# Stick-breaking attention heads: the running sum's row copied by ScalarE straight into the operand, in place of a copy by ScalarE and one by GpSimd

## What is computed

```python
z = jnp.einsum('bqhd,bkhd->bhqk', q_blk, kh).astype(jnp.float32) * scale
mask = key_pos[None, :] < q_pos[:, None]
log_1m_beta = jnp.where(mask, jax.nn.log_sigmoid(-z), 0.0)
between = lax.cumsum(log_1m_beta, axis=3, reverse=True) - log_1m_beta
weights = jnp.where(mask, jnp.exp(jax.nn.log_sigmoid(z) + between), 0.0)
return jnp.einsum('bhqk,bkhd->bqhd', weights.astype(vh.dtype), vh)
```

## Time and profile before

| | us |
|---|---|
| median of three runs | 1421.17 |
| the three runs | 1421.07, 1421.17, 1424.47 |
| profiled execution | 1422.15 |
| its span | 1420.4 |
| mean granted TensorE clock | 0.985 |

### The profile page before, as it was taken

One profiled execution on the slowest core, in us unless ns is written; L12 is line 12 of the kernel. 1 busy time (PEld: TensorE's weight loads), 2 busy tenths in 40 slices (PEclk: granted clock), 3 DMA queues, 4 the chain that ended last, 5 costly groups with the idle time before them and its releaser, 6 DMA issues.

```text
span 1420.4 us, 27700 instructions
## 1 busy us (share of the span) xinstructions
PE 1355.1 (95%) x11020; PEld 1062.2 (75%) x11020; DVE 873.6 (61%) x1347; ACT 676.3 (48%) x1249; POOL 322.2 (23%) x434
## 2 busy tenths in 40 slices
PE   6999989999899999998999889999999999999997
PEld 5877767877677665655578678888888888888886
DVE  6245261475753465667376787766766656668866
ACT  5533241252523487978464544454444434345541
POOL 6675544532332042435103100000000000000000
PEclk9999999999999899999999999999999999999999
DMA  6555333522325330403253254454444865787952
GB/s 206 148 156 151 104 82 89 152 67 72 95 75 126 124 77 2 91 2 121 85 180 104 82 161 145 147 163 148 156 141 161 294 198 175 253 277 246 298 193 112
DMA packets 191546, 201.07 MB, mean 142 GB/s; under 512 B 36669, under 2 KB 127994, under 8 KB 191418
## 3 DMA queue, kind: packets, MB, share of 16 engines
q1 hardware_dynamic: 145132, 169.47, 37.8%
q10 hardware_dynamic: 46286, 29.84, 7.5%
HBM read 145.06 MB, written 54.20 MB: 140 GB/s over the span
## 4 chain that ended last, share of the span: by engine, by line
PE 44%; DVE 3%; ACT 1%; DMA 1%; issue 1%; DVEq 0%; SPq 0%; ACTq 0%
PE all_ps_b L2670 20%; PE all_ps_b L2661 19%; PE all_ps_b L1669 4%; DMA pl_slot<-in_w_out 1%; PE all_ps_b L2617 0%; DMA pl_xt<-in_w_ff 0%; DVE ro_slot L2325 0%; DVE pl_hH L2511 0%; DVE pl_hL L2511 0%; DVE ro_hT L2325 0%; DVE pl_y L2305 0%; DVE pl_y L2307 0%; DVE ro_wo L2329 0%; ACT pl_hL L2239 0%; DVE pl_xt L2349 0%
## 5 line engine op out<-in xcount | busy, mean ns | idle before, releaser
L484 POOL TENSOR_TENSOR fr_wL<-fr_raw,fr_wH 128x256 fp32r<-128x256 f32 (+1 forms) x208 | 162.5, 812 | 75.1 <-PE fr_ps_F L1278 53.8
L1278 PE MATMUL fr_ps_F<-fr_hL,fr_wH 128*128 128x512 f32 (+1 forms) x416 | 168.2, 404 | 2.9 <-DVE fr_hL L805 2.4
L1278 PE MATMUL fr_ps_F<-fr_hH,fr_wH 128*128 128x512 f32 (+1 forms) x416 | 166.1, 399 | 0.0
L1278 PE MATMUL fr_ps_F<-fr_hH,fr_wL 128*128 128x512 f32 (+1 forms) x416 | 111.6, 397 | 0.7 <-POOL fr_wL L484 0.7
L2661 PE MATMUL all_ps_b<-ro_hH,ro_slot 128*128 128x512 f32 x272 | 89.7, 397 | 5.9 <-ACT pl_raw L2139 5.9
L1278 PEld LDWEIGHTS fr_ps_F<-fr_hL,fr_wH 128*128 128x128 f32 (+1 forms) x416 | 76.6, 184 | 22.8 <-issue 3.1
L1278 PEld LDWEIGHTS fr_ps_F<-fr_hH,fr_wL 128*128 128x128 f32 (+1 forms) x416 | 75.1, 184 | 19.9 <-issue 1.5
L1278 PEld LDWEIGHTS fr_ps_F<-fr_hH,fr_wH 128*128 128x128 f32 (+1 forms) x416 | 76.7, 184 | 17.6 <-issue 1.3
L478 POOL CAST fr_wH<-fr_raw 128x1024 fp32r<-128x1024 f32 (+1 forms) x42 | 47.5, 1130 | 161.2 <-PE fr_ps_F L1278 141.1
L2670 PE MATMUL all_ps_b<-ro_hH 128*128 128x512 f32 x312 | 75.9, 389 | 0.0
L2670 PE MATMUL all_ps_b<-ro_y 128*128 128x512 f32 x300 | 72.7, 390 | 0.5 <-DVE ro_y L2489 0.5
(11 more groups left out here) (483 smaller groups left out, 3114.7 us busy)
## 6 DMA issues: line engine op xcount, KB each, us to landing
pl_slot<-in_w_ff SPq DMA_DIRECT2D x88, 256.0 KB, 4.5
pl_slot<-second_operands SPq DMA_DIRECT2D x75, 256.0 KB, 3.6
fr_raw<-in_w_in ACTq DMA_DIRECT2D x37, 512.0 KB, 4.2
second_operands<-pl_hL SPq DMA_DIRECT2D x64, 256.0 KB, 2.0
pl_hT<-in_w_ff SPq DMA_DIRECT2D x44, 256.0 KB, 4.6
projected<-fr_stage ACTq DMA_DIRECT2D x39, 256.0 KB, 4.4
pl_hT<-second_operands SPq DMA_DIRECT2D x37, 256.0 KB, 3.7
pl_xt<-in_w_ff SPq DMA_DIRECT2D x16, 512.0 KB, 5.6
```

The costliest lines, as they stand in the source:

```text
L484: m = pool.tensor_tensor(wL[b][:, k:k + 2, 0:wd], raw[b][:, k:k + 2, 0:wd], wH[b][:, k:k + 2, 0:wd].bitcast(F32), ALU.subtract)
L1278: m = pe.matmul(F[b][0:wd, :], w[b][:, k, 0:wd], a[:, k, :], start=(at_ == 0), stop=(at_ == len(passes) - 1))
```

## The change

The row buffers are gone. ScalarE copies row 0 of the bank straight into row 0 of `SP[(u + 2) % 4]`. For that it has to wait until the softplus of unit u+2 is done (`sp`), since that one writes the same buffer. The copy's place in ScalarE's queue moves: it was between the weight of unit u and the Exp of unit u+3, and is now between the Exp and the Ln of unit u+3. In the last units of a pair, where there is no unit u+3, it stands right behind the weight. The semaphore `handed` is gone; the scores wait for `placed`, at the same counts. GpSimd keeps its other work and has no row copies.

```diff
-        row = [r.sb(f"row{n}", [1, HALF]) for n in range(4)]
@@ GpSimd
                     if not first:
-                        known = UNITS[u - 2][3]
-                        pool.wait_ge(s("handed"), handed(i, u - 2))
-                        pool.wait_ge(s("sp"), i * NU + u + 1)
-                        pool.tensor_copy(SP[u % 4][0:1, known:HALF], row[(u - 2) % 4][0:1, known:HALF]
-                                         ).then_inc(s("placed"), 1)
                         gla(i * NG + NTH[u] - 1)
@@ ScalarE
             def logs(i, u):
+                exponential(i, u)
+                logarithm(i, u)
+
+            def exponential(i, u):
                 act.wait_ge(s("z"), i * NU + u + 1)
                 if u >= 4 or i:
                     act.wait_ge(s("tri_mm"), i * NU + u - 3)
                 act.activation(part(E[u % 4], u), part(Z[u % NZ], u), ACT.Exp).then_inc(s("exp"), 1)
+
+            def logarithm(i, u):
                 act.wait_ge(s("exp"), i * NU + u + 1)
                 act.activation(part(E[u % 4], u), part(E[u % 4], u), ACT.Ln, bias=1.0).then_inc(s("log"), 1)
...
                 def hand_on(u):
 
                     off = UNITS[u][3]
-                    if u >= 4 and hands_on(u - 4):
-
-                        act.wait_ge(s("placed"), placed(i, u - 2))
-                    act.copy(row[u % 4][0:1, off:HALF], Z[u % NZ][0:1, off:HALF]).then_inc(s("handed"), 1)
+                    act.wait_ge(s("sp"), i * NU + u + 3)
+                    act.copy(SP[(u + 2) % 4][0:1, off:HALF], Z[u % NZ][0:1, off:HALF]).then_inc(s("placed"), 1)
 
                 for u in range(NU):
                     weight(u)
-                    if hands_on(u):
-                        hand_on(u)
                     if u + AHEAD < NU:
-                        logs(i, u + AHEAD)
+                        exponential(i, u + AHEAD)
+                        if hands_on(u):
+                            hand_on(u)
+                        logarithm(i, u + AHEAD)
                     elif i < LAST and u == NU - 1:
                         for n in range(AHEAD):
                             logs(i + 1, n)
+                    if hands_on(u) and u + AHEAD >= NU:
+                        hand_on(u)
@@ TensorE, scores
                     if u >= NZ and hands_on(u - NZ):
-                        pe.wait_ge(s("handed"), handed(i, u - NZ))
+                        pe.wait_ge(s("placed"), handed(i, u - NZ))
```

## The result

| | before | after |
|---|---|---|
| median, us (4 runs each) | 1422.07 (1421.07 to 1424.47) | 1439.67 (1436.6 to 1441.59) |
| ratio | | 1.0128 (95%: 1.0105 to 1.0151) |
| profiled execution, its span | 1422.15, 1420.4 | 1441.59, 1439.9 |
| start of the first weight to the end of the last ("the stage" below) | 200.8 | 216.1 |
| from the span's start to the first weight | 484.4 | 489.5 |

The account below looks back on a forecast made before the run. No single engine is the limit; the unit's loop of waits (sums, weight, row and PSUM bank back to TensorE) is. Walks 7.8 + 5 - 2 - 1.3 = +9.5, taken as +9 on 1421.17: 1430.2 us, range 1415 to 1444.

Parts of the forecast that it names:

- faster (1): TensorE's lead absorbs the late banks and ScalarE's overlap of copy and Exp counts: -7 us, 1414 us; chance 0.18.
- no change (2): Gains of 4 to 6 us cancel against as much loss, or the copy's place makes no difference: 1421 us; chance 0.20.
- The full lock step: Every late bank holds because TensorE's lead over ScalarE is gone: 37.2 less 10 of gains, +27 us, 1448 us; chance 0.10.
- its clause on the clock: More TensorE gaps could bring more stretches at 1.2 of 2.4 GHz, where work takes double; counted within the +27 us rival.
- The 3.3 us: Gains booked: 2 us outside the walks by GpSimd's going, 1.3 us from the row copy ahead of each pair's last sums.
- the 37.2 us of late banks: First-order upper bound of loss: 48 of 66 units get their PSUM bank back late for the scores, nothing absorbed.
- the four walks: Four stretches traced by moving each instruction to its latest predecessor; they cover 17.5 us of late banks and give 7.8 us.
- the remaining 19.7 us: Late banks outside the walks, taken as mostly small units, 0.1 to 0.6 us each; a quarter let through, 5 us.
- walk a: Pair 0, units 12 to 16: row copy held by VectorE's softplus; sums 2.9 us later at unit 16, of 3.9 first order.
- walk b: Pair 0, units 21 to 26: late softplus and bank, gate's Exp and VectorE's gate step delayed; 2.7 us, of 4.3.
- walk c: Pair 1, units 16 to 20: row copies of units 16 and 19 held by the softplus; 2.1 us lost, of 2.8.
- walk d: Pair 2, units 16 to 24: score slips of 1 us and less, 1.02 us regained from GpSimd; 0 lost, of 6.5.

Follow-up runs that it names:

- h_rowfirst: The kernel before with ScalarE's row copy ahead of the weight of the same unit; 1.0008 (0.9989 to 1.0028) of before.
- a_order: The kernel before with ScalarE's row copy moved between Exp and Ln, GpSimd still placing the row, no softplus wait; 1.0016, stage +4.3 us.
- j_after_late: The kernel after with VectorE's linear-attention pieces one unit later in its queue; 1.0061 of before, stage 207.7 us.
- c_twostep: The kernel after with two ScalarE copies: bank to row buffer behind the weight, then to the operand with the softplus wait; 1.0147, stage +18.8 us.
- e_again: The kernel before with a second ScalarE copy of each row, to an unread spare, without a softplus wait; 1.0053, stage +7.0 us.
- d_banklate: The kernel before with the scores waiting until GpSimd has placed the row, not until ScalarE has copied it out; 1.0114, stage +16.4 us.

## Why the prediction had the sign and the mechanism, and not the size

The steps that held. The bound: no engine is full, and the way back of the bank matters. The overlap of copy and Exp is there, 0.47 and 0.47 for 0.61 us. The row is almost never late for the sums: TensorE waits for the copy with its sums once, 0.4 us, where it waited 2.6 us for GpSimd's. The last units were forecast at 2.2 to 2.3 us each and took 2.24. The waits for the bank (21.3 us) and for the softplus (17.9) are as large as was said, though the softplus holds the copy in 18 places and not in 29. Of the rivals, faster (1) and no change (2) fell. The full lock step, +27 us (3), did not happen either, but 17.6 lies about midway between it and the +9 forecast, and its clause on the clock was not idle: the lower clock that after shows from about 538 to 541 us, behind TensorE's wait of 2.06 us, has no counterpart in before, and over the stage TensorE is busy for 2.4 us more. The 3.3 us that the prediction booked as gained by GpSimd's going no run isolates; h_rowfirst, which gives GpSimd its row earlier, gained nothing. Of the two rules of the Trainium skill that were weighed, the one on consistent bubbles (Perfetto Trace Analysis, "Optimization Strategy") agrees with the trace: the score product's wait for its bank is such a bubble, 30 times. The one on the shared port pair (SBUF — State Buffer, "SBUF: two separate sides") would have had VectorE gain by the 72 copies gone; in the stage VectorE's busy time did fall from 127.1 to 119.8 us, and no time came of it.

The step that failed is the last one of the sum, how much of the 37.2 us of late banks comes through. The prediction had 7.8 us from the four walks (they add to 7.7, and the 0.5 us of the last four units is in neither), which cover 17.5 us, and let a quarter of the remaining 19.7 us through, 5 us, less 3.3 us of gains. I compare the weights' starts of the two traces, each counted from the first weight:

| stretch | predicted | measured |
|---|---|---|
| walk a, pair 0, units 12 to 16 | +2.9 | +2.3 |
| walk b, pair 0, units 21 to 26 | +2.7 | +1.6 |
| walk c, pair 1, units 16 to 20 | +2.1 | +0.2 |
| walk d, pair 2, units 16 to 27 | 0 | -0.9 |
| all that was not walked | +1.7 | +12.1 |
| sum | +9.4 (taken as +9) | +15.3 |

The walks were too high, not too low, though c depends on where one stops: to the weight of unit 21 it is +1.6. That the sum isn't further off is luck in part: the walks' excess of 4.5 us stood against a shortfall of 10.4 in the rest. The loss came from what was only estimated: 3.5 us in units 16 to 21 of pair 0 (the places shown above; 2.45 of it come at the weight of unit 19, in the second round), 2.6 us in units 5 to 8 of pair 1, where the copy of unit 6 (ScalarE in after)

```profile
584.71 0.47 ACT L3399 COPY sb_E<-all_ps_b 1x386 f32<-1x386 f32 x1 [1.54 <-DVE sb_E L3484]
```

waits for a softplus that stands behind the linear attention's last steps, 2.1 us in the end of pair 1 and 2.5 us in the first 16 units of pair 2. I had called the rest "mostly small units, 0.1 to 0.6 us at a time, where TensorE has gaps". That reading of the rows was wrong. By the prediction's own rule, some 14 of these 19.7 us lie in 12 places of 0.85 to 2.1 us each, 9 of them in full units: 4 us in units 20 to 23 of pair 0, and 2.1 us at unit 10 of pair 1, whose bank comes back from the copy of unit 6 shown here. In 7 of the 12 it is the softplus that holds the copy, the pattern of walks a and b, and the quarter was a guess without a row.

Underneath lies a point of method. The first-order sum put two costs into one number. The move behind the Exp made banks late by 21.1 us in the rows of before and cost 4.3 us in a_order, a fifth: TensorE's lead takes it up, as rival 1 said. The wait for the softplus made them later by 16 us more, and cost 11: two thirds. The wait closes a loop through two queues, and with the loop broken (j_after_late) 8.4 us of the stage came back. These shares are differences between kernels and hold only if the two costs add. One fraction for both could not fit. The walks had seen this loop (walk b names the gate's Exp, VectorE's gate step, the next softplus and the next copy), but the sum did not make use of it.

What stays open: how the 11 us divide between the stall on ScalarE, the bank, and the lower clock of some executions. Each alone costs 12 to 16 us (c_twostep against e_again, d_banklate), together 15; no kernel here waits for the softplus with neither, and d_banklate was not run with VectorE's move. The 5.1 us ahead of the stage in the profiled execution of after are taken as scatter, which was not shown.

## What to carry to other kernels

A copy that is moved from an idle engine to a busy one takes its waits along, and there they hold back everything queued behind. Before costing such a move, list for each wait what the awaited engine may itself be waiting for: if that is something queued behind the waiting instruction, the wait closes a loop, and its cost can be paid in each round, though none of the engines is full. And sum the costs of a moved place and of an added wait apart, since slack can take up the one and not the other.

## What the runs showed of the hardware

The 1 by 512 copy out of PSUM takes ScalarE 0.56 us, the same as a copy of 128 by 512 out of PSUM in the same stage, and an Exp of 128 by 512 takes 0.58: the number of partitions made no difference.

```profile
590.20 0.56 ACT L2944 COPY gla_vnat<-all_ps_b 128x512 f32<-128x512 f32 x1
```

Where nothing holds it, a ScalarE instruction starts about 0.1 us before the end of the one ahead, also a copy between an Exp and the Ln that waits for that Exp (698.11, 698.58, 699.05); only a direct successor that needs the result starts 0.03 us after the end in place of 0.1 us before it. The Trainium skill (ScalarE: Activation LUTs, "What ACT_TABLE_LOAD costs") says that ACTIVATEs back to back overlap by about 93 ns; the trace, with 0.09 to 0.12 us, agrees. What VectorE waits for matters more than its load: it was busy for 119.8 of 216.1 us in the stage, 55%, while ScalarE waited for its softplus in 18 places, 1 us on the mean and 2.5 at most. In after the granted clock was at its lower level, 0.50 of full speed (1.2 GHz), from 538 to 540 us, right after TensorE had been idle for 2.06 us (537.74), and the sums took 1.91 us there (538.63) where they take 1.12 us in the last pair (696.45).
